# Order of small matmuls among the parts of the array: one transformer block on one Trainium2 core

## What is computed

```
w = -softplus(-(w0 + tanh(xw) @ w2)) - 0.5            # decay, from a 64-wide input
decay = exp(-exp(w))
a = sigmoid(a0 + xa @ a2)                             # rate, from a 64-wide input
kk = k * k_k;  kk = kk / max(sqrt(sum_head(kk*kk)), 1e-12)
k = k * (1 + (a - 1) * k_a)
step: sa = state @ (-kk);  state = state*decay + sa (x) (kk*a) + v (x) k;  y = state @ r
mean = mean_head(y);  var = mean_head((y-mean)^2)
y = (y-mean) * rsqrt(var + eps) * gain + bias + bonus;  y = y * g
```

## Time and profile before

| | us |
|---|---|
| median of 3 runs | 1986.86 (1985.1 to 1989.57) |
| profiled execution | 1986.76 |
| its span in the trace | 1985.0 |
| PE busy | 1939.5 (98%) |
| DVE busy | 1049.0 (53%) |
| ACT busy | 849.4 (43%) |

### The profile page before, as it was taken

How to read it: one execution, slowest core, us unless ns; L and a number is a source line. 1 busy time by engine, 2 the same in 40 slices (tenths; PEclk the granted TensorE clock), 3 DMA queues, 4 the chain that set the end, 5 groups by cost and what they waited for, 6 DMA issues and landing times.

```text
span 1985.0 us, 29402 instructions
## 1 busy us (share of the span) xinstructions
PE 1939.5 (98%) x11105; PEld 1646.5 (83%) x11105; DVE 1049.0 (53%) x1098; ACT 849.4 (43%) x964; POOL 11.0 (1%) x23
## 2 busy tenths in 40 slices
PE   8999999999999999999999799999999999999997
PEld 7888888888888889999999578888888888888886
DVE  5445444544444445788556735554444444544443
ACT  6444444444344446634432435544444444434443
POOL 1000000000000000000000000000000000000000
PEclk9999999999999999999999799999999999999998
DMA  7666666666666667554622246666666666666663
GB/s 237 191 191 190 190 190 190 190 182 189 190 191 192 190 197 235 154 150 126 185 85 78 99 126 183 211 191 190 189 187 186 190 190 190 190 187 196 191 193 125
DMA packets 194920, 353.60 MB, mean 178 GB/s; under 512 B 23760, under 2 KB 26064, under 8 KB 194576
## 3 DMA queue, kind: packets, MB, share of 16 engines
q1 hardware_dynamic: 194144, 352.23, 60.0%
q0 software_dynamic: 512, 0.06, 0.0%
q10 hardware_dynamic: 176, 0.07, 0.0%
HBM read 346.56 MB, written 5.77 MB: 177 GB/s over the span
## 4 chain that ended last, share of the span: by engine, by line
PE 93%; DVE 4%; DMA 1%; ACT 1%; issue 1%; SPq 0%; ACTq 0%; DVEq 0%
PE psA L314 39%; PE psB L314 38%; PE psB L730 5%; PE psA L730 4%; PE psT L555 1%; DVE wlo L299 1%; DMA raw<-in_w_in 1%; DMA x<-in_x 0%; DVE subst L922 0%; PE psM L1085 0%; DVE tinv L922 0%; PE psA L741 0%; PE psT L1067 0%; ACT whi L290 0%; DVE y L922 0%
## 5 line engine op out<-in xcount | busy, mean ns | idle before, releaser
L299 DVE TENSOR_TENSOR wlo<-raw,whi 128x1024 fp32r<-128x1024 f32 (+1 forms) x648 | 788.1, 1218 | 842.3 <-ACT whi L290 836.6
L290 ACT CAST whi<-raw 128x1024 fp32r<-128x1024 f32 (+1 forms) x648 | 676.6, 1046 | 955.9 <-PE psA L314 448.4
L314 PE MATMUL psA<-whi,xh 128*128 128x512 f32 (+1 forms) x736 | 283.9, 386 | 0.0
L314 PE MATMUL psA<-whi,xl 128*128 128x512 f32 (+1 forms) x736 | 283.4, 385 | 0.0
L314 PE MATMUL psA<-wlo,xh 128*128 128x512 f32 (+1 forms) x736 | 283.3, 385 | 0.0
L314 PE MATMUL psB<-whi,xh 128*128 128x512 f32 x704 | 275.9, 392 | 0.0
L314 PE MATMUL psB<-whi,xl 128*128 128x512 f32 x704 | 274.2, 389 | 0.0
L314 PE MATMUL psB<-wlo,xh 128*128 128x512 f32 x704 | 274.2, 389 | 0.0
L314 PEld LDWEIGHTS psA<-whi,xh 128*128 128x128 f32 x736 | 138.5, 188 | 27.4
L314 PEld LDWEIGHTS psA<-wlo,xh 128*128 128x128 f32 x736 | 138.5, 188 | 27.4
L314 PEld LDWEIGHTS psA<-whi,xl 128*128 128x128 f32 x736 | 138.4, 188 | 27.5
(11 more groups left out here) (373 smaller groups left out, 2190.4 us busy)
## 6 DMA issues: line engine op xcount, KB each, us to landing
raw<-in_ffn_w_gate SPq DMA_DIRECT2D x176, 512.0 KB, 3.7
raw<-in_ffn_w_up SPq DMA_DIRECT2D x176, 512.0 KB, 3.7
raw<-in_ffn_w_down SPq DMA_DIRECT2D x176, 512.0 KB, 3.7
raw<-in_w_in SPq DMA_DIRECT2D x80, 512.0 KB, 3.7
raw<-in_w_out SPq DMA_DIRECT2D x32, 512.0 KB, 3.7
x<-in_x SPq DMA_DIRECT2D x4, 512.0 KB, 7.4
x_dram<-x SPq DMA_DIRECT2D x4, 512.0 KB, 8.6
x<-x_dram SPq DMA_DIRECT2D x4, 512.0 KB, 6.7
```

The costliest lines, as they stand in the source:

```text
L290: nc.scalar.copy(whi[:, slot, :, 0:ncol], raw[:, slot, :, 0:ncol]).then_inc(hi_ready, 1)
L299: nc.vector.tensor_tensor(wlo[:, slot, :, 0:ncol], raw[:, slot, :, 0:ncol], whi[:, slot, :, 0:ncol].bitcast(F32), ALU.subtract).then_inc(l ...
L314: mm = nc.tensor.matmul(ps[:, tb, 0:ncol], lhs[:, k0 + t, tok], rhs[:, slot, t, 0:ncol], start=(first and t == 0 and p == 0), stop=(last a ...
```

## The change

Same products, in another order, and two tables in another layout.

- `z` and `za` are no longer apart: `decay_and_rate(i)` fills half i of both at a time, in turn: rows 0 to 63, then 64 to 127. The half 0 of both stands where `z` stood, the half 1 where `za` stood. `rounds` and ACT's program follow.
- `head_sums` writes to four strips of 32 columns in turn, each with two of the eight tiles summed; the numbers of the heads now lie in 64 of 128 partitions (four each in groups of 32), so DVE and ACT work on `hstat` over all partitions.
- `spread` reads four strips of 32 rows in turn, each writing to another PSUM bank.
- `state_maps`, the scan's three steps: `par` (and in `state_maps` the half) is now the inner loop.

```
-            channel_rounds("z", lambda t: lora_w[0:64, t * P:(t + 1) * P], lora_wa[0:64, 0, :])
+            decay_and_rate(0)
             win_groups(15, 17)
-            channel_rounds("za", lambda t: lora_w[64:P, t * P:(t + 1) * P], lora_wa[64:P, 0, :])
+            decay_and_rate(1)
...
+        def decay_and_rate(i):
+            pz, pa = fill("z", i), fill("za", i)
+            for t in range(4):
+                at = slice((4 * i + t) * P, (4 * i + t + 1) * P)
+                last_z = T.matmul(pz[:, t * S:(t + 1) * S], lora_w[0:64, at], lora_wa[0:64, 0, :], start=True, stop=True)
+                if t == 3:
+                    filled(last_z)
+                last_a = T.matmul(pa[:, t * S:(t + 1) * S], lora_w[64:P, at], lora_wa[64:P, 0, :], start=True, stop=True)
+            filled(last_a)
...
         def spread(name, stat):
-            for i in range(2):
-                ps = fill(name, i)
-                for t in range(4):
-                    mm = T.matmul(ps[:, t * S:(t + 1) * S], to_channels[0:RH, 4 * i + t, :], stat[0:RH, 2, :],
-                                  start=True, stop=True)
-                filled(mm)
+            both = fill(name, 0), fill(name, 1)
+            for odd in range(2):
+                for quad in range(4):
+                    t, rows_ = 2 * quad + odd, slice(32 * quad, 32 * quad + 32)
+                    mm = T.matmul(both[t // 4][:, t % 4 * S:(t % 4 + 1) * S], to_channels[rows_, t, :],
+                                  stat[rows_, 2, :], start=True, stop=True)
+                    if odd and quad % 2:
+                        filled(mm)
...
         def head_sums(name, src):
             ps = fill(name, 0)
-            for t in range(NT):
-                mm = T.matmul(ps[0:RH, 0:S], to_heads[:, t, :], src[:, t, :], start=(t == 0), stop=(t == NT - 1))
+            for odd in range(2):
+                for quad in range(4):
+                    mm = T.matmul(ps[32 * quad:32 * quad + 32, 0:S], to_heads[:, odd, :], src[:, 2 * quad + odd, :],
+                                  start=(odd == 0), stop=(odd == 1))
...
-                for half in range(2):
-                    hs = slice(64 * half, 64 * half + 64)
-                    for jj in range(RH):
-                        par, t = jj // NT, jj % NT
-                        mm = T.matmul(ps[64 * par:64 * par + 64, half * COLS + t * C:half * COLS + (t + 1) * C],
+                for t in range(NT):
+                    for par in range(2):
+                        jj = par * NT + t
+                        for half in range(2):
...
+        def head_pairs():
+            for t in range(NT):
+                for par in range(2):
+                    yield t, par * NT + t, slice(64 * par, 64 * par + 64)
...
-            for jj in range(RH):
-                par, t = jj // NT, jj % NT
-                ch = slice(64 * par, 64 * par + 64)
-                out_ = ps[ch, t * C:(t + 1) * C]
-                T.matmul(out_, b_tok[hs, blk, hcol(jj)], sa_of(c)[hs, jj * C:(jj + 1) * C], start=True, stop=False)
-                mm = T.matmul(out_, k_tok[hs, blk, hcol(jj)], v_tok[hs, blk, hcol(jj)], start=False, stop=True)
+            for t in range(NT):
+                for par in range(2):
+                    jj = par * NT + t
+                    T.matmul(ps[64 * par:64 * par + 64, t * C:(t + 1) * C], b_tok[hs, blk, hcol(jj)],
+                             sa_of(c)[hs, jj * C:(jj + 1) * C], start=True, stop=False)
+                for par in range(2):
+                    jj = par * NT + t
+                    mm = T.matmul(ps[64 * par:64 * par + 64, t * C:(t + 1) * C], k_tok[hs, blk, hcol(jj)],
+                                  v_tok[hs, blk, hcol(jj)], start=False, stop=True)
```

More of the change, by code:

```diff
@@ L73, in constants @@
     t[:, 128:256] = p[:, None] // 64 == p[None, :] // 64
-    head = 2 * np.arange(NT)[:, None] + (p // 64)[None, :]
-    t[:, 256:384] = (head.T[:, :, None] == np.arange(RH)).reshape(P, NT * RH)
+    for odd in range(2):
+        t[:, 256 + 32 * odd:288 + 32 * odd] = 2 * odd + (p // 64)[:, None] == np.arange(32)[None, :]
     t[:, 384:448] = np.arange(C)[None, :] > (p % 64)[:, None]
@@ L93, in constants @@
     rotary(P, 32, 1280)
-    t[0:RH, 1792:2816] = (head[None, :, :] == np.arange(RH)[:, None, None]).reshape(RH, NT * P)
+    for i in range(NT):
+        rows_ = slice(32 * (i // 2), 32 * (i // 2) + 32)
+        t[rows_, 1792 + P * i:1792 + P * (i + 1)] = np.arange(32)[:, None] == 2 * (i % 2) + (p // 64)[None, :]
     return t
@@ L123, in build @@
         same_head = consts[:, 128:256]
[L124 removed]
+        to_heads = consts[:, 256:320].rearrange("p (t h) -> p t h", h=32)
         mask2 = consts[:, 384:512]
@@ L852, in build @@
         PAIRS = (pA, pB, pT, pM)
-        rounds = [("scale", 0), ("small", 0), ("z", 0), ("z", 1), ("za", 0), ("za", 1), ("kn", 0), ("kb", 0), ("kb", 1),
+        rounds = [("scale", 0), ("small", 0), ("z", 0), ("za", 0), ("z", 1), ("za", 1), ("kn", 0), ("kb", 0), ("kb", 1),
                   ("b0", 0), ("b0", 1), ("k0", 0), ("k0", 1), ("at", 0), ("at", 1), ("bonus", 0), ("bonus", 1),
@@ L1220, in win_dve @@
             ps = full(V, "kn", 0)
-            vread(V.tensor_scalar(hstat[0:RH, 0, :], ps[0:RH, 0:S], 1e-24, None, ALU.max), "kn", 0)
+            vread(V.tensor_scalar(hstat[:, 0, :], ps[:, 0:S], 1e-24, None, ALU.max), "kn", 0)
             splits(33, 34)
             need(V, "kk_root")
-            vdone(V.reciprocal(hstat[0:RH, 2, :], hstat[0:RH, 1, :]), "kk_inv")
+            vdone(V.reciprocal(hstat[:, 2, :], hstat[:, 1, :]), "kk_inv")
             splits(34, 36)
@@ L1364, in win_act @@
             sigmoids("z", sw, "w0", 0)
-            splits(18, 19)
+            sigmoids("za", iclr, "a0", 0)
+            splits(18, 20)
             sigmoids("z", sw, "w0", 1)
-            splits(19, 20)
-            sigmoids("za", iclr, "a0", 0)
+            sigmoids("za", iclr, "a0", 1)
             splits(20, 21)
-            sigmoids("za", iclr, "a0", 1)
             splits(21, 23)
@@ L1384, in win_act @@
             stored(A, "kn", 0)
-            adone(A.activation(hstat[0:RH, 1, :], hstat[0:RH, 0, :], ACT.Sqrt), "kk_root")
+            adone(A.activation(hstat[:, 1, :], hstat[:, 0, :], ACT.Sqrt), "kk_root")
             splits(33, 44)
@@ L1495, in rwkv_dve @@
             ps = full(V, "var", 0)
-            vread(V.tensor_scalar(hstat_gn[0:RH, 0, :], ps[0:RH, 0:S], 1.0 / C, GN_EPS, ALU.mult, ALU.add), "var", 0)
+            vread(V.tensor_scalar(hstat_gn[:, 0, :], ps[:, 0:S], 1.0 / C, GN_EPS, ALU.mult, ALU.add), "var", 0)
             in_out(NCH - 1)
@@ L1523, in rwkv_act @@
             stored(A, "var", 0)
-            adone(A.activation(hstat_gn[0:RH, 1, :], hstat_gn[0:RH, 0, :], ACT.Sqrt), "gn_root")
+            adone(A.activation(hstat_gn[:, 1, :], hstat_gn[:, 0, :], ACT.Sqrt), "gn_root")
             split_hi(w0_out, 0, 0, 3)
@@ L1652, in scan_sa_pe @@
             ps = fill("sa", c)
-            for jj in range(RH):
-                par, t = jj // NT, jj % NT
-                ch = slice(64 * par, 64 * par + 64)
+            for t, jj, ch in head_pairs():
                 mm = T.matmul(ps[hs, jj * C:(jj + 1) * C],
@@ L1682, in scan_y_pe @@
                 state = states[(c - 1) % 2]
-                for jj in range(RH):
-                    par, t = jj // NT, jj % NT
-                    ch = slice(64 * par, 64 * par + 64)
+                for t, jj, ch in head_pairs():
                     T.matmul(ps[ch, t * C:(t + 1) * C], state[ch, t, :], r[ch, t, c * C:(c + 1) * C],
                              start=True, stop=True)
[L1688 to L1694, removed]
+            for t in range(NT):
+                for par in range(2):
+                    jj = par * NT + t
+                    T.matmul(ps[64 * par:64 * par + 64, COLS + t * C:COLS + (t + 1) * C],
+                             sa_of(c)[hs, jj * C:(jj + 1) * C], bx1[hs, blk * RH + jj, :], start=True, stop=False)
+                for par in range(2):
+                    jj = par * NT + t
+                    mm = T.matmul(ps[64 * par:64 * par + 64, COLS + t * C:COLS + (t + 1) * C],
+                                  v_tok[hs, blk, hcol(jj)], kx1[hs, blk * RH + jj, :], start=False, stop=True)
             filled(mm)
```

10 lines of the change are left out of this document (5 added, 5 removed).

## The result

The changed kernel took 1959.61 us (median of 4 runs, 1958.37 to 1960.66), the kernel before 1986.49 us beside it. The ratio is 0.9866, with a 95% interval of 0.9851 to 0.9881: 27 us faster. The profiled execution took 1958.37 us, its span is 1956.6 us.

A forecast was written before the change was run, and what follows sets the result against it. PE was taken to bound the kernel. Its gains of 35.1 us, less 2.4, 2.4 and 0.3 not reaching the end, left 30.0; less 1.0 for the clock, 29.0: from 1986.76 to 1958 us, range 1952 to 1967.

The forecast's parts named there:

- price list: Start-to-start step of small matmul passes on PE: two parts of the array in turn halve it, four parts quarter it.
- two terms for which no row of before had the shape: Head sums on four column strips, 2.5 us each; column halves on fixed rows, 4.8 us in `st`, 6.4 in `ys`.
- The clock behind `kb`: Right behind `kb`, the granted clock no longer falls to half: 1.6 us gained, the other end 0.
- What didn't reach the end: Gains on PE lost in waits: 2.4 us at `vb`, 2.4 at the last `ys`, 0.3 at `wlo` behind the rates.
- wait at group 28: Behind the rates, PE comes earlier than DVE's `wlo`; the next splits are late by some 0.3 us.
- Rival A: Weight splits on ACT and DVE set the pace behind the rates and in the scan: 5 to 7 us, 1964; chance 0.15.
- The term of the clock before `mean`: A 4.6 us wait before `mean` lets the clock fall; cost 1 to 1.7 us, counted as 1.0 at three in four.
- rival D: Nothing is lost to the clock and DVE: the whole 33 us is kept, 1953; chance 0.10.
- B: Columns alone don't overlap: `st`, second part of `ys`, `kn` and `var` keep their times; 14.6 us go, 1972; chance 0.10.
- C: Array must empty when only the column half changes: 0.218 us a pass in seven rounds, about 2044; chance 0.03.

## Why the prediction was right

**The steps.** The price list held: half for two parts, a quarter for four, whichever of rows and columns alternates. The two terms for which no row of before had the shape came out at the end I had taken: four column strips with 128 rows take 1.00 us for 16 passes, and fixed rows with alternating column halves take 2.01 us a round, which the run with the old order confirmed at the end of the program. The floor of about 25 ns from start to start (the Trainium skill, "TensorE: Matmul & The Clock Gate", section "Wait — 56ns, not 53.3ns?") isn't met here either: `gt` steps by 2.02/128 = 16 ns. The 2.38 times of the Trainium skill for three column strips (same page, Part 3) isn't contradicted by the 3.56 times (3.56 us against 1.00) of four here, but a sum by it would have been 0.6 us short for each head sum.

**The clock behind `kb`.** `kb` to `b0` went from 19.73 to 15.66 us: 4.1, forecast 2.4 + 1.6. That the rows in use decide it the prediction had only as an expectation; the experiment on all rows and the bursts listed there bear it out.

**What didn't reach the end.** `vb` gave nothing: with `spread` on all rows it takes 2 us longer and PE's wait behind it falls from 7.8 to 6.0 us. The last `ys` gave nothing. `var` was passed on in full: from `var` (25.6) to `g` (28.2) the lead grew by 2.6 us. The wait at group 28 is printed as 0.32 us, forecast 0.3, but that agreement is luck: late `wlo` cost 0.8 us in all at groups 27 to 29, since DVE came 1.5 us earlier and not 2.4. Rival A, the weight splits, still fell: PE's waits for `wlo` come to 3.7 us in the whole program, and at A's other places, the scan around `sa` of chunk 1 and the systems, there is none.

**Where sizes were off.**
- The term of the clock before `mean` was put at 1.0, from 1 to 1.7 us at three in four. It fell as forecast, but lay low for 5.1 us of `mean`, where the earlier trace rows shows 3.5 us of work at the low clock; `mean` took 2.5 us longer, 2.1 of them at the end. In four executions with the same wait the loss was 1.4 to 1.7 us, inside the range.
- A wait of 1.2 us at the index rounds wasn't in the sum. I had followed DVE only up to the last `sa` and checked who waits for `sa` and `state`, but not who waits for the buffer: `idx` of the third quarter fills the buffer that `st` of chunk 0 had filled, and DVE reads that behind the scores. The 0.7 us for `wlo` of group 85 was in the text, as part of the wait before `mean`.
- `z` and `za` gave 2.6 where 3.4 were taken from PE and 3.3 were forecast to be kept.
- PE waits less for `wlo` in the substitution: 2.6 us where it was 4.1. I had left it unchanged. This is chance and no effect of the change, since the same kernel waits 4.2 us in its other execution. It makes up for what `z` and `za` and the stall in `k0` (0.8 here) took: `gt` is 11.7 us earlier, where 9.8 and the head start of 1.8 were due.
- The time given for rival D is 1 us off: 1986.76 - 33 is 1954 and not 1953.

In sum 29.0 forecast for the profiled execution, 28.4 measured, of which 1.8 belong to the pair and not to the change; 1958 forecast, 1959.6 measured. That the profiled gain comes within 0.6 us is luck. From `z` to the turned probabilities, with the head start left out, the gain is 26.4 us in one execution of the changed kernel and 25.4 in the other, so the sum was 2.6 to 3.6 us too high. The mechanism and the price list were right; what was too high is what was left over behind the waits.

**The rivals.** B and C fell with `st` at 2.01 us a round. D fell by the clock and the index wait. A, as said.

## What to carry to other kernels

If two loops over small matmuls commute, let the part of the array change at least every second matmul (shown here for float32, 64 by 64 and on strips of 32 rows); the step from start to start, not the duration or the busy share, shows whether it does. Look for the same shape in an order that alternates already: its step is the price. When PE becomes faster in a fixed order, list for every buffer who reads it and where that reader stands in its own program; the waits that appear are cheap to mend by moving work into the idle time that the other engine had before.

## What the runs showed that I had not expected

- Passes of up to four parts start together, even when the program has them two by two: `kb` 1.10 us against 1.08. With runs of four, `gt` needs 2.57 us a round instead of 0.98, with runs of eight 3.17. How this comes about inside PE stays open.
- The granted clock fell in or right behind bursts on 16 rows, four times of four, and stayed up behind bursts as long on 64 or 128 rows, twelve times of twelve (`g` left out, as said above). Why the rows count the runs don't show.
- It fell behind the 1.2 us wait of the index rounds in three of the nine executions that have this wait (5.3 instead of 4.36 us for `ys` and `idx`), with the same work before it and the same wait. The next `sa` came 1.5 us later in these three, the turned probabilities 0.9 us, since `mean` then took 4.8 us and not 5.6. So such a wait can cost 0.9 us more than its length, and what decides it these runs don't show.
- The same unchanged instructions take up to 1.5 us more or less in the substitution and up to 2.7 us behind the turned probabilities from one execution to the next. Differences of that size between two whole times say little; the distance from a fixed place in the trace says more.
- The stall inside `k0`, 0.2 to 1.6 us in the nine kernels in which the rounds ahead of it are changed and none in the two in which they aren't, stays unexplained; it takes back a part of the gain.
